# The first norm moves into the first attention's block: rows turned unscaled, keys, queries and values multiplied afterwards

## What is computed

```python
u = rmsnorm(x, attn_norm_g)      # x * rsqrt(mean(x*x) + eps) * g, a root for each token, a gain for each column
q_sb, k_sb, v_sb, c_q, c_kv, k_rope = split(u @ w_in)
# first attention ("stick breaking"), 8 heads of 64: z = q.k / 8, strictly causal,
# a = exp(log_sigmoid(z) - (sum of softplus(z) over the keys between)),  out = a @ v
# latent attention from rmsnorm(c_q), rmsnorm(c_kv) and the rotated k_rope
```

## Time and profile before

| | us |
|---|---|
| three runs of the kernel before | 3813.42, 3818.93, 3811.29 |
| their median | 3813.42 |
| profiled execution: its time | 3811.53 |
| its span in the profile | 3809.7 |
| the norm stage, up to the first dense matmul | 33.44 |
| first attention, up to the latent stage's first load | 399.49 |

### The profile page before, as it was taken

One profiled execution on the slowest core, in us unless ns is written; L12 is line 12 of the kernel. 1 busy time (PEld: TensorE's weight loads), 2 busy tenths in 40 slices (PEclk: granted clock), 3 DMA queues, 4 the chain that ended last, 5 costly groups with the idle time before them and its releaser, 6 DMA issues. The chain is left out here.

```text
span 3809.7 us, 48006 instructions
## 1 busy us (share of the span) xinstructions
PE 3613.5 (95%) x17243; PEld 2948.4 (77%) x17243; DVE 1819.7 (48%) x3405; ACT 1217.8 (32%) x2273; POOL 1340.2 (35%) x800
## 2 busy tenths in 40 slices
PE   7987788999999999999999999997999999999997
PEld 6776667888888887788888888886788676868686
DVE  4656455244444445566666666666404324242422
ACT  4777244110000003445555555556101202020200
POOL 3210210243333322565555665563232131313331
PEclk9998899999999999999999999998999999999998
DMA  3000210211111113533322432221413020202231
GB/s 94 23 6 6 53 31 29 94 61 45 50 50 50 45 39 78 54 48 51 55 50 46 38 40 39 36 36 52 153 45 106 28 72 23 78 23 72 99 127 68
DMA packets 201140, 208.77 MB, mean 55 GB/s; under 512 B 12479, under 2 KB 155886, under 8 KB 200958
## 3 DMA queue, kind: packets, MB, share of 16 engines
q1 hardware_dynamic: 181390, 155.23, 18.6%
q10 hardware_dynamic: 19568, 50.93, 3.7%
HBM read 174.61 MB, written 31.52 MB: 54 GB/s over the span
## 5 line engine op out<-in xcount | busy, mean ns | idle before, releaser
L868 PE MATMUL ps<-all_u_hi,kept_w_hi 128*128 128x512 f32 x1824 | 731.4, 401 | 15.6 <-POOL kept_w_lo L824 15.6
L872 PE MATMUL ps<-all_u_hi,kept_w_lo 128*128 128x512 f32 x1824 | 712.9, 391 | 0.0
L871 PE MATMUL ps<-all_u_lo,kept_w_hi 128*128 128x512 f32 x1824 | 711.8, 390 | 0.0
L822 POOL CAST kept_w_hi<-kept_w_raw 128x1024 fp32r<-128x1024 f32 x116 | 129.7, 1118 | 1281.4 <-PE ps L868 715.0
L1529 POOL TENSOR_SCALAR even_probs<-even_probs,even_stat 128x640 f32<-128x640 f32 (+1 forms) x250 | 428.0, 1717 | 349.7 <-DVE even_stat L1965 349.7
L868 PEld LDWEIGHTS ps<-all_u_hi,kept_w_hi 128*128 128x128 f32 x1824 | 344.6, 189 | 77.8 <-POOL kept_w_lo L824 15.8
L872 PEld LDWEIGHTS ps<-all_u_hi,kept_w_lo 128*128 128x128 f32 x1824 | 342.9, 188 | 73.7
L871 PEld LDWEIGHTS ps<-all_u_lo,kept_w_hi 128*128 128x128 f32 x1824 | 344.0, 189 | 62.6
L1781 ACT ACTIVATE even_probs<-even_probs,even_stat 128x128 f32<-128x128 f32 (+7 forms) x256 | 199.1, 778 | 302.0 <-DVE even_stat L1959 302.0
L824 POOL TENSOR_TENSOR kept_w_lo<-kept_w_raw,kept_w_hi 128x1024 fp32r<-128x1024 f32 x116 | 283.3, 2442 | 9.3
L868 PE MATMUL ps<-kept_w_hi,all_u_hi 128*128 128x512 f32 x640 | 252.5, 395 | 7.8 <-DVEq L2842 7.8
(11 more groups left out here) (411 smaller groups left out, 7483.9 us busy)
## 6 DMA issues: line engine op xcount, KB each, us to landing
kept_w_raw<-in_even_w_in_dram SPq DMA_DIRECT2D x64, 512.0 KB, 8.1
kept_w_raw<-in_odd_w_in_dram SPq DMA_DIRECT2D x48, 512.0 KB, 3.8
kept_w_raw<-in_w_up_dram SPq DMA_DIRECT2D x16, 512.0 KB, 4.0
mlp_w_raw<-in_w_up_dram SPq DMA_DIRECT2D x16, 512.0 KB, 4.1
kept_w_raw<-in_w_down_dram SPq DMA_DIRECT2D x16, 512.0 KB, 3.5
mlp_w_raw<-in_w_down_dram SPq DMA_DIRECT2D x16, 512.0 KB, 3.5
scratch_h<-residual SPq DMA_DIRECT2D x8, 1024.0 KB, 4.5
residual<-scratch_negc ACTq DMA_DIRECT2D x16, 512.0 KB, 5.8
```

Of the source, the lines that this page charges most:

```text
L822: nc.gpsimd.tensor_copy(hi, raw).then_inc(w_hi.sem, 1)
L868: ins = nc.tensor.matmul(dst, lh, rh, start=first, stop=False)
L871: nc.tensor.matmul(dst, lh, rl, start=False, stop=False)
L872: return nc.tensor.matmul(dst, ll, rh, start=False, stop=last)
```

## The change

The norm's block is gone. SyncE's loads, the squares, the turning and the roots stand in the first attention's block. Its tiles for x are the memory that the attention uses later for the next keys, queries, values, V, softplus and Y. Rows are turned unscaled by transposes as soon as they arrive (the first half of the tokens after two 1 MB tiles), the second half between the matmuls of the first unit. The first weight unit is loaded between the second and the third tile of x. POOL clears its two key areas first, splits unit 0 when it has arrived, and units 1 and 2 only after the eight diagonals. After the first unit TensorE spreads the roots, and ScalarE copies them into R.

POOL then multiplies each pair's keys, queries and values (128x1024 each, after ScalarE has taken them) by R, and everything that waited for ScalarE's copy of them waits for this product. For the first pair ScalarE's copies stand one take later: keys' after the fourth half, queries' after the sixth. In the latent stage ScalarE's copy into C gets the root as a scale, and VectorE multiplies each half of KR by R.

The diff, cut to its core:

```diff
-    def stick_stage(stage, rounds, weight, bases, w):
+    def stick_stage(stage, rounds, weight, bases, w, src, gain_vectors):
...
+        xs = sb("x", [P, TT, SEQ])
+        KN, QN, VN = (xs[:, i, :] for i in range(3))
...
             @block.sync
+                for i, g in enumerate(gain_vectors):
+                    sp.dma_start(gain_rows[i * KT:(i + 1) * KT, :], g.rearrange("(k p) -> k p", p=P))...
+                rows_in(0)
+                rows_in(1)
+                w_load(sp, w, 0, per, 0, cols(weight, bases[0]))
+                rows_in(2)
+                rows_in(3)
+                for u in range(1, per):
+                    w_load(sp, w, 0, per, u, cols(weight, bases[u]))
...
             @block.gpsimd
+                def scaled(p, i):
+                    if p >= rounds:
+                        return
+                    pool.wait_ge(dense_out.sem, dense_out.at(ND * p + 2 * i + 2))
+                    pool.sem_inc(w_go.sem, 1)
+                    nc.gpsimd.tensor_tensor(NEXT[i], NEXT[i], R[:], ALU.mult).then_inc(scaled_in.sem, 1)
+                    pool.wait_ge(scaled_in.sem, scaled_in.at(3 * p + i + 1))
...
-                    pool.wait_ge(dense_out.sem, dense_out.at(ND * p + 2))      # split_keys
+                    pool.wait_ge(scaled_in.sem, scaled_in.at(3 * p + 1))
...
+                w_open_pool(pool, w)
+                w_split(pool, w, 0, per, 0, fresh=True)
+                pool.wait_ge(turn_scaled.sem, turn_scaled.at(TT))
+                w_split(pool, w, 0, per, 1, fresh=True)
+                w_split(pool, w, 0, per, 2, fresh=True)
+                pool.wait_ge(spread_out.sem, spread_out.at(1))
+                scaled(0, 0)
                 split_keys(0, 0)
+                scaled(0, 1)
                 split(1, 0)
+                scaled(0, 2)
                 split_keys(0, 1)
                 split(1, 1)
+                scaled(1, 0)
                 split(1, 2)
                 for p in range(1, rounds):
+                    scaled(p, 1)
                     split(p + 1, 0)
                     split_keys(p, 0)
+                    scaled(p, 2)
                     split(p + 1, 1)
                     split_keys(p, 1)
+                    scaled(p + 1, 0)
                     split(p + 1, 2)
...
             @block.tensor
                     for k in (2 * piece, 2 * piece + 1):
+                        if turning:
+                            turn_arrived(pe, half, k)
                         last = product(...)
+                        if turning and half == 0:
+                            turn_arriving(KT + k)
...
-                    pe.wait_ge(dense_out.sem, dense_out.at(ND * p + ND))       # turn_v
+                    pe.wait_ge(scaled_in.sem, scaled_in.at(3 * p + 3))
...
+                for n in range(KT):
+                    turn_arriving(n)
                 for e in range(4 * ND):
+                    if e == 8:
+                        turn_spread(pe)
+                    eighth(0, e, ps[:, e // 4, :], e < 8)
...
             @block.scalar
-                    act.wait_ge(dense_out.sem, dense_out.at(ND * p + 2 + 2 * i))   # split_of
+                    act.wait_ge(scaled_in.sem, scaled_in.at(3 * p + 1 + i))
...
+                squared(0)
+                squared(2)
+                turn_act(act, GAIN_ATTN, between={6: lambda: squared(4), 8: lambda: squared(6)}, root_at=10)
                 for n in range(ND):
                     take_half(0, n, ps[:, n, :])
-                    if n == 1:
+                    if n == 3:
                         split_of(0, 0, 0)
-                    elif n == 3:
+                    elif n == 5:
                         split_of(0, 0, 1)
...
             @block.vector
+                squared(1)
+                squared(3)
+                turn_dve_arriving(dve, GAIN_ATTN, {6: lambda: squared(5), 8: lambda: squared(7)})
...
     low_stage:
-                    nc.scalar.activation(C[:, t, :], ps[:, 6 + t % 2, 0:3 * P], ACT.Copy).then_inc(hi_done.sem, 1)
+                    nc.scalar.activation(C[:, t, :], ps[:, 6 + t % 2, 0:3 * P], ACT.Copy, scale=ROOT[:, t:t + 1])...
...
                     step(nc.vector.tensor_tensor(KR[:, at], A[:, at], B[:, at], ALU.add))
+                    step(nc.vector.tensor_tensor(KR[:, at], KR[:, at], R[:, at], ALU.mult))
```

More of the change, by code:

```diff
@@ L173, in program @@
     saved = sem("saved")
+    scaled_in = sem("scaled_in")
     rows_hi_done = sem("rows_hi_done")
@@ L687, in turn_spread, with turn_act @@
         last.then_inc(spread_done.sem, 1)
-    def turn_act(act, gain, twice=False):
+    def turn_act(act, gain, twice=False, between={}, root_at=1):
         v, ln = roots[:, 2, :], roots[:, 3, :]
@@ L698, in turn_act @@
         for n in range(2 * KT):
-            if n == 1:
+            if n in between:
+                between[n]()
+            if n == root_at:
                 root_of(0, FIRST_ROOT if twice else ROOT)
@@ L756, in turn_dve, with turn_dve_arriving, lo_of, turn_close @@
                 .then_inc(turn_scaled.sem, 1)
-    def turn_close(twice=False):
+    def turn_dve_arriving(dve, gain, between):
+        v, q = roots[:, 2, :], roots[:, 4, :]
+        def lo_of(n):
+            k = gain.start + n % KT
+            dve.wait_ge(hi_done.sem, hi_done.at(n + 1))
+            nc.vector.scalar_tensor_tensor(out=UL[turn_place(n)], in0=turn_bank(n), scalar=gain_cols[:, k:k + 1],
+                                           in1=UH[turn_place(n)].bitcast(F32), op0=ALU.mult, op1=ALU.subtract)\
+                .then_inc(lo_done.sem, 1)
+        for n in range(2 * KT):
+            if n in between:
+                between[n]()
+            lo_of(n)
+            if n == KT:
+                dve.wait_ge(squares.sem, squares.at(TT // 2))
+                dve.wait_ge(squares_dve.sem, squares_dve.at(TT // 2))
+                nc.vector.tensor_scalar(v, sums[:, 0, :], 1.0 / D, EPS, ALU.mult, ALU.add).then_inc(turn_mean.sem, 1)
+            if n == KT + 2:
+                dve.wait_ge(turn_root.sem, turn_root.at(1))
+                dve.wait_ge(turn_mean.sem, turn_mean.at(1))
+                nc.vector.tensor_tensor(q, ROOT, ROOT, ALU.mult).then_inc(turn_newton.sem, 1)
+                dve.wait_ge(turn_newton.sem, turn_newton.at(1))
+                nc.vector.tensor_tensor(q, q, v, ALU.mult).then_inc(turn_newton.sem, 1)
+                dve.wait_ge(turn_newton.sem, turn_newton.at(2))
+                nc.vector.tensor_scalar(q, q, -0.5, 1.5, ALU.mult, ALU.add).then_inc(turn_newton.sem, 1)
+                dve.wait_ge(turn_newton.sem, turn_newton.at(3))
+                nc.vector.tensor_tensor(ROOT, ROOT, q, ALU.mult).then_inc(turn_newton.sem, 1)
+                dve.wait_ge(turn_newton.sem, turn_newton.at(4))
+        for t in range(TT):
+            nc.vector.tensor_scalar(R[:, t * P:t * P + P], ident[:], ROOT[:, t:t + 1], None, ALU.mult)\
+                .then_inc(turn_scaled.sem, 1)
+    def turn_close(twice=False, newtons=5):
         for m in (turned, hi_done, lo_done):
@@ L763, in turn_close @@
             m.close(2 if twice else 1)
-        turn_newton.close(12 if twice else 5)
+        turn_newton.close(12 if twice else newtons)
         spread_done.close(1)
@@ L1077, in _, with eighth @@
             def _(pe):
-                def eighth(p, e, dst):
+                def eighth(p, e, dst, turning=False):
                     n, piece = e // 4, e % 4
@@ L1353, in stick_stage @@
         v_turned.close(2 * rounds)
+        turn_close(newtons=4)
+        scaled_in.close(3 * rounds)
+        gain_in.close(16 * len(gain_vectors))
+        gain_turned.close(1)
+        gain_out.close(1)
+        squares.close(TT // 2)
+        squares_dve.close(TT // 2)
+        for m in tile_in:
+            m.close(16)
         v_out_dve.close(2 * rounds)
@@ L2230, in _ @@
                     at = slice(half * HALF, half * HALF + HALF)
-                    b = 19 + 3 * half
+                    b = 19 + 4 * half
                     dve.wait_ge(dense_done.sem, dense_done.at(7 + half))
@@ L2249, in low_stage @@
         step_act.close(2)
-        step_dve.close(25)
+        step_dve.close(27)
         ctx.close()
@@ L3418, in program @@
     held, w = weights_for("sb", 3)
-    turn_norm_stage("n1", [(0, D, flat(attn_norm_g))], src=x2, hi=UH, lo=UL, ahead=(w, 3, pair_unit(one(w_in), bases)),
-               opening=False, more=(flat(mlp_norm_g), final_norm_g, flat(even_norm), flat(odd_norm)))
-    stick_stage("sb", SB_HEADS // 2, one(w_in), bases, w)
+    stick_stage("sb", SB_HEADS // 2, one(w_in), bases, w, x2,
+                (flat(attn_norm_g), flat(mlp_norm_g), final_norm_g, flat(even_norm), flat(odd_norm)))
     held.close()
```

47 lines of the change are left out of this document (41 added, 6 removed).

## The result

The changed kernel takes 3823.97 us (median of 13 runs, 3815.87 to 3825.47), the kernel before 3813.15 in the 13 runs beside them. The ratio is 1.0023, 95% interval 1.0016 to 1.0031: 8.8 us slower (0.0023 x 3813), between 6.1 and 11.8. That is inside the predicted range, and 4.6 us above the forecast's 3819.4. It is at the very edge of the forecast's own range of 3814 to 3824. It is on the slower side of the 0.2% border, which had 0.43.

A forecast was written before the change was run, and what follows sets the result against it. TensorE, busy 95% of the span, was taken as the bound. Opening -4.9, values +8.2, queries +2.1 and latent stage +0.6 made +6.0 us on 3811.53, or 3819.4 set against the runs' median; range 3809 to 3828.

The forecast's parts named there:

- the forecast's own range: Whole kernel: 3814 to 3824 us for the case that all terms hold as summed, chance 0.52.
- the 0.2% border: Whole kernel: 7.6 us either way is what a measurement can tell; chance 0.43 of lying above the upper border, 3821.0.
- Opening, -4.9: First attention's opening: first scores at 61.4 instead of 67.05, 5.65 us gained, less 0.75 given back; ends -9.5 and -2.
- I take 0.75: VectorE's first scans: POOL's later splits run into them, a delay of 0.5 to 1.7 costing 0.2 to 1.4 us.
- Values, +8.2: Three later V turnings: TensorE waits for POOL's multiplication, 3.0 us later each, less 0.8; ends +5 and +12.5.
- the prediction's two readings: V turnings: 8.2 us if VectorE's scan locks POOL out for its whole instruction, nearer 7 with shared bandwidth.
- Queries, +2.1: Later pairs' query copies: ScalarE stalls 0.7 us behind POOL's multiplication, three times; ends 0 and +5.
- Keys, 0: Later pairs' keys and POOL's order: the work stays hidden, the tightest place holding by a microsecond before scores at 139.0.
- Latent stage, +0.6: Latent stage: ScalarE's eight copies get a column as scale, 0.07 us dearer each; VectorE's k_rope multiplications cost 0.
- Half clock: V turnings and opening: TensorE runs at half clock behind the longer wait, total 3825.6 us; chance 0.20.
- Covered: V turnings: downstream idle time absorbs the stall and VectorE isn't held in the opening, -3.3 us, 3810; chance 0.16.
- Opening that doesn't move: Opening: half clock or VectorE's order sets a first unit at 35 or later; gain 2 to 3, total 3822; chance 0.12.

The follow-up runs named there:

- opening_only: Changed kernel without POOL's multiplications for head pairs 2 to 4, their waits back at the dense products; 3811.47 us, ratio 0.9996 to the kernel before.
- v_in_copy: Changed kernel with the values' root of pairs 2 to 4 multiplied in VectorE's copy of the turned values, not by POOL; 3808.4 us, 0.9984 of the kernel before.
- q_early: Changed kernel with ScalarE splitting the first pair's queries after the opening's fifth take instead of the sixth; 3818.02 us, ratio 1.0010 to the kernel before.
- v_only: Kernel before, with POOL multiplying only the values of pairs 2 to 4 by ones and TensorE waiting for it; 3821.26 us, ratio 1.0019.
- kq_only: Kernel before, with POOL multiplying only keys and queries of pairs 2 to 4 by ones, in the changed kernel's order; 3815.99 us, ratio 1.0006.
- keys_first: Changed kernel with POOL splitting the first head's keys before the next pair's unit, not after; 3823.22 us, ratio 1.0027 to the kernel before.
- third_late: Kernel before with one POOL wait added: the next pair's third weight unit is split only after that pair's keys are taken; 3812.99 us, ratio 1.0001.
- v_third_early: Changed kernel with values' roots in VectorE's copy, and the third unit's split put back ahead of the next keys' multiplication; 3807.14 us, 0.9984 of the kernel before.
- v_q: Changed kernel with values' roots in VectorE's copy and the first queries split after the fifth take; 3804.66 us, ratio 0.9972 to the kernel before.
- v_q_free: v_q without POOL's wait for the scaled diagonals ahead of the opening's second unit; 3804.97 us, ratio 0.9975 to the kernel before.
- mul_only: Kernel before with its norm, POOL multiplying keys, queries and values of pairs 2 to 4 by ones, with the changed kernel's waits; 3824.21 us, ratio 1.0030.

## Why the prediction was right, and where it was off

**Opening, -4.9: the mis-sized term.** Its landmarks came as worked out: first dense product 17.99 (17.5), second unit at 34.83 (34.9), first scores 61.32 (61.4), 5.73 earlier (5.65). Only the second unit's releaser is not as forecast: POOL's split ended at 34.62, and TensorE, busy with the spread of the roots from 33.13 on, didn't wait for it. What failed is the step "I take 0.75" for what is given back at once. By 94 us the trace had given back 3.0 (5.73 to 2.74), and opening_only came out at -1.5 (-5.0 to +1.9) with the latent stage in it, against the prediction's -4.3; that the term was too large rests on the traces, as the interval holds both. Two things were not in the sum. The wait ahead of the first scores put them at the lower clock level; the prediction priced the 4.5 us only as a delay. And the first scan, which I knew would meet POOL, lost 1.7 us (3.18 against 1.49) on the path of the first V turning: POOL's work on the first keys and the next unit had stood at 52.8 to 60.9 in the kernel before, under dense products, and now queues behind the V multiplication to 68.1. v_in_copy and q_early remove one of these each.

**Values, +8.2: right.** v_only gives +7.2 (3.8 to 10.7), the changed kernel's trace 7.0, and each wait was 4.4 against a forecast of 4.5 to 4.8. The scan holds POOL for less of it than the prediction had:

```profile
153.78 1.76 DVE L1426 TENSOR_TENSOR_SCAN sb_later_long<-sb_x 128x768 f32<-128x768 f32 x1
155.10 2.58 POOL L1097 TENSOR_TENSOR sb_x<-sb_x,all_roots_spread 128x1024 f32<-128x1024 f32 x1 [15.19 <-ACT sb_x L1288]
...
157.74 1.11 PE L1178 MATMUL ps<-all_ident,sb_x 128*128 128x128 f32 x4 [4.43 <-POOL sb_x L1097]
```

The instruction is shown as starting at 155.10, right behind ScalarE's take (154.94) and still inside the scan, which ends at 155.54. It ends 2.14 after the scan and lasts 2.58, where POOL alone takes 2.34 to 2.41: held for 0.2 us, not for the rest of the scan and then a whole instruction. So this row lies between the prediction's two readings (8.2 by the lock, nearer 7 without) and doesn't choose. The lock itself shows better elsewhere: a scan of 1.76 that lasts 3.60 behind a subtraction that keeps its 2.35, and the query low half at 58.45, which ends 1.07 us after POOL's 59.99, lasting 2.61 instead of 1.22. This is what the Trainium skill states ("SBUF — State Buffer", section "Who interferes with whom"): an exclusive lock of the pair, for a whole instruction.

**Queries, +2.1: the mechanism right, the size by the trace 1.5.** ScalarE's wait is 0.50 each time (0.7 forecast). That kq_only gives +2.3 (-1.1 to +5.7) is in part luck: its trace is +2.4 at the stage's end, but by spells of both signs (+3.2 at 115 to 125, -3.3 at the second V turning, where its order also moves the split away, +5.9 behind 343), not by three times 0.7.

**Keys, 0: off in one place.** POOL's multiplication, unit split and key split filled 126.00 to 139.92, and the last was stretched by VectorE's scans:

```profile
135.70 4.22 POOL L1124 TENSOR_TENSOR sb_k_lo<-sb_x,sb_k_hi_hi 64x1024 fp32r<-64x1024 f32 x1
140.18 0.47 PE L1196 MATMUL ps<-sb_k_hi_hi,sb_q_hi_lo 128*128 128x512 f32 x1 [1.65 <-POOL sb_k_lo L1124]
```

"It holds by a microsecond" took POOL's durations without the lock that the same working had established: the three took 13.9 us where it counted 11. It failed in one pair, by 1.65 us, and keys_first shows that it doesn't decide.

**Latent stage, +0.6:** from the table load to the end the changed trace loses 12.5 - 11.05 = 1.4 us. Its first product waits 16.71 for POOL's split of a kept unit, 15.59 before, and ScalarE's C copies take 1.05 a pair against 0.88, which makes the forecast's term, 0.5 in all. The 1.1 us of the longer first wait were not in the sum. No run took this apart.

**The rivals.** Half clock: its mark came (1.11 us for four turnings at 157.74), but the kernel before was already at the lower level soon behind that place, and v_only's +7.2 (10.7 at most) is short of the 12.4 that it wants for the values. In the changed kernel TensorE is busy 1.5 us longer over the three turnings, where it wants 4.2. It is also the case whose total, 3825.6, came nearest to the measured one, by the opening's loss and by clock in other stretches (3.3 us of the trace), which no rival had. Covered: falls with v_only, since the V waits stay in full. Opening that doesn't move: it moved; only its gain was small, 1.5 where this rival gave 2 to 3.

## What to carry to other kernels

A factor belongs in a copy that exists: the values' roots cost 7 us as an instruction of POOL between a product and its reader (v_in_copy is 15 faster than the changed kernel, but 2.7 of that is the opening and part of it clock), and VectorE's copy out of PSUM took them at its old 0.68 us. An opening made shorter shows its worth only at the first instruction that nothing else delays: here every engine's work that lay hidden under the old opening (the query copy, the key splits) had to move with it. And when TensorE is stopped just ahead of a dense stretch, price the stretch behind the stop too.

## What the runs showed of the hardware that I had not expected

The last stretch, from the fourth V turning to the table load, holds the same 289 matmuls in every kernel, with at most two instructions of POOL. It lasted (length, TensorE busy, PEclk among the columns) in opening_only, where it is as long as in the kernel before, in v_only, v_in_copy and the changed kernel:

```profile
317.93:395.44 77.51, 54.52 (x289) 48.46 (x289) 42.97 (x47) 49.97 (x91) 0.00 (x0) 0.70 0.05 14
```

```profile
331.22:410.08 78.86, 56.49 (x289) 50.65 (x289) 41.59 (x45) 48.42 (x88) 3.38 (x2) 0.65 0.05 14
```

```profile
312.93:393.29 80.36, 56.98 (x289) 50.77 (x289) 42.89 (x47) 50.42 (x91) 0.00 (x0) 0.67 0.05 14
```

```profile
326.60:410.56 83.96, 61.49 (x289) 54.75 (x289) 41.58 (x45) 48.73 (x88) 3.40 (x2) 0.62 0.05 13
```

The idle time is the same within 1.0 us (22.4 to 23.4); the busy time for the same instructions differs by 7.0 us between the first and the last, and that is the granted clock. Half of the extra 12.5 us of the changed kernel's profiled execution lies here, in a stretch into which the change puts no multiplication.

It is not chance of one trace, though. The thirteen traces fall into groups by what POOL multiplies for pairs 2 to 4. Nothing (the kernel before, opening_only, third_late): 77.5 us each. The values alone (v_only): 78.9. Keys and queries, without POOL's multiplication of the values (kq_only, v_in_copy, v_third_early, v_q, v_q_free): 80.4 each. All three (the changed kernel, keys_first, q_early): 84.0 each. Only mul_only falls out, 80.4 with all three. Within a group the lengths agree to 0.1 us, while the stretch begins up to 11 us apart. So by the traces the multiplications cost up to 6.5 us through the clock, in a stretch that holds none of them. By what path they set the pattern of the two levels stays open; no run varied it.

Open too is why the second half of the second pair's V turning ran at the upper level in v_third_early and at the lower in the kernel before, behind nearly the same waits (1.68 and 1.55; 1.68 and 0.69). Such spells are worth up to 3 us each, as much as a removed wait. And one execution can mislead: third_late, 4.9 us ahead at the stage's end in its trace, was traced in the fastest of its eleven runs (3807.10) and is level in the median. q_early's and v_q_free's traces are of their slowest.
